# The turn between two halves of a state-space scan: from VectorE to ScalarE, and the second halves half a step later

## What is computed

```
abar = exp(dt * a)                       # per state, complex
s[t] = abar * s[t-1] + bu[t]             # a scan over 256 tokens, complex
y = Re(C s) + d * u;  y = gelu(y)
```

```
first_re = z_re[127]*cos128 - z_im[127]*sin128
first_im = z_im[127]*cos128 + z_re[127]*sin128
```

## Time and profile before

| | |
|---|---|
| time of three runs | 3233.09 us (median), 3228.68 and 3240.85 |
| the profiled execution | 3230.05 us |
| its span | 3228.7 us, 48855 instructions |
| busy: TensorE, VectorE, ScalarE, GpSimd | 3064.6, 2135.8, 1376.7, 307.3 us |
| chain that ended last | TensorE 77%, VectorE 11%, DMA 7%, ScalarE 2% |
| DMA | 632.08 MB, mean 196 GB/s |

### The profile page before, as it was taken

One profiled execution on the slowest core, in us unless ns is written; L12 is line 12 of the kernel. 1 busy time (PEld: TensorE's weight loads), 2 busy tenths in 40 slices (PEclk: granted clock), 3 DMA queues, 4 the chain that ended last, 5 costly groups with the idle time before them and its releaser, 6 DMA issues.

```text
span 3228.7 us, 48855 instructions
## 1 busy us (share of the span) xinstructions
PE 3064.6 (95%) x20283; PEld 2762.3 (86%) x20283; DVE 2135.8 (66%) x2568; ACT 1376.7 (43%) x1682; POOL 307.3 (10%) x255
## 2 busy tenths in 40 slices
PE   5799988998899999999998999999999999999998
PEld 1588878898888888888998999999999888888887
DVE  6689996677777554655787776666455755555555
ACT  2233323333353443434455564544444544444343
POOL 4547650000000000000000000000000100000000
PEclk8899999999999999999999999999999999999999
DMA  8855558867767666566555555445555556565664
GB/s 302 276 173 164 164 174 276 278 229 254 254 198 271 189 194 191 186 197 188 177 158 170 170 176 164 147 151 161 177 189 170 178 188 186 194 192 191 189 190 155
DMA packets 311483, 632.08 MB, mean 196 GB/s; under 512 B 30096, under 2 KB 34816, under 8 KB 310624
## 3 DMA queue, kind: packets, MB, share of 16 engines
q1 hardware_dynamic: 298496, 618.74, 59.4%
q10 hardware_dynamic: 11904, 5.61, 0.6%
q0 software_dynamic: 864, 4.60, 0.5%
HBM read 624.66 MB, written 4.21 MB: 195 GB/s over the span
## 4 chain that ended last, share of the span: by engine, by line
PE 77%; DVE 11%; DMA 7%; ACT 2%; issue 2%; ACTq 1%; SPq 0%; DVEq 0%
PE PS L918 13%; PE PS L905 12%; PE PS L906 11%; PE PS L907 11%; PE PS L922 7%; PE PS L934 6%; PE PS L936 6%; PE PS L935 6%; DVE wlo L1743 3%; DMA raw<-in_w_in 2%; ACT whi L2257 2%; DVE aacc L1732 2%; DMA raw<-in_w_ada 1%; DMA raw<-in_w_proj_attn 1%; DMA raw<-in_w_out 1%
## 5 line engine op out<-in xcount | busy, mean ns | idle before, releaser
L1743 DVE TENSOR_TENSOR wlo<-raw,whi 128x1024 fp32r<-128x1024 f32 x983 | 1244.4, 1270 | 920.9 <-ACT whi L2257 919.5
L2257 ACT ACTIVATE whi<-raw 128x1024 fp32r<-128x1024 f32 x983 | 1036.0, 1058 | 1386.7 <-PE PS L907 503.6
L905 PE MATMUL PS<-R,whi 128*128 128x256 f32 x4160 | 1209.5, 291 | 57.0 <-DVE wlo L1743 38.2
L906 PE MATMUL PS<-R,whi 128*128 128x256 f32 x4160 | 1189.4, 286 | 0.0
L907 PE MATMUL PS<-R,wlo 128*128 128x256 f32 x4160 | 1189.0, 286 | 0.0
L905 PEld LDWEIGHTS PS<-R,whi 128*128 128x128 f32 x4160 | 810.5, 195 | 99.4 <-issue 47.0
L906 PEld LDWEIGHTS PS<-R,whi 128*128 128x128 f32 x4160 | 811.0, 195 | 0.8 <-issue 0.7
L907 PEld LDWEIGHTS PS<-R,wlo 128*128 128x128 f32 x4160 | 810.2, 195 | 0.0
L918 PE MATMUL PS<-R,whi 128*128 128x512 f32 x1920 | 484.7, 395 | 14.7 <-DVE R L1660 8.6
L918 PEld LDWEIGHTS PS<-R,whi 128*128 128x128 f32 x1920 | 348.0, 190 | 78.6 <-issue 15.4
L934 PE MATMUL PS<-whi,R 128*128 128x512 f32 x896 | 350.1, 391 | 1.6 <-issue 0.9
(11 more groups left out here) (356 smaller groups left out, 1833.8 us busy)
## 6 DMA issues: line engine op xcount, KB each, us to landing
raw<-in_w_in SPq DMA_DIRECT2D x295, 512.0 KB, 4.1
raw<-in_w_ff SPq DMA_DIRECT2D x256, 512.0 KB, 4.0
raw<-in_w_ada SPq DMA_DIRECT2D x175, 512.0 KB, 4.8
raw<-in_w_mlp_up SPq DMA_DIRECT2D x128, 512.0 KB, 4.1
raw<-in_w_mlp_down SPq DMA_DIRECT2D x128, 512.0 KB, 3.9
raw<-in_w_out SPq DMA_DIRECT2D x64, 512.0 KB, 4.3
raw<-in_w_rnn_proj SPq DMA_DIRECT2D x32, 512.0 KB, 3.6
raw<-in_w_attn_proj SPq DMA_DIRECT2D x32, 512.0 KB, 3.7
```

The source lines that it names most:

```text
L905: pe.matmul(o, whi[:, s, c:c + P], x.operand.hi(k), start=first, stop=False, skip_group_check=True)
L906: pe.matmul(o, whi[:, s, c:c + P], x.operand.lo(k), start=False, stop=False, skip_group_check=True)
L1743: v.tensor_tensor(wlo[:, i % SPN, :], words(j), whi[:, i % SPN, :].bitcast(F32), ALU.subtract).then_inc(lo_done, 1)
L2257: a.activation(whi[:, i % SPN, :], words(j), ACT.Copy).then_inc(hi_done, 1)
```

## The change

The turn is made by ScalarE, in a side job of its own (`ssm` in the scalar program), in the even phase 2k+4: two multiplications by `-sin128` and `sin128`, then, after a wait for them, two multiply-adds with `cos128`, all on one column. It waits for the first scans (`half_done`) and signals `first_done`. VectorE's second scans of step k move from the end of the odd phase 2k+3 to the start of the even phase 2k+4, after that tick's L1743 and before the rotation of step k+1, and wait for `first_done`. GpSimd makes `-sin128` as well, one more subtraction in each half of the tables, behind a wait for VectorE's parameters, since the tile `b_` is used by these before. Nothing in TensorE's, SyncE's or GpSimd's side jobs of the stage is changed. The whole diff:

```diff
--- before.py
+++ after.py
@@ -259,7 +259,7 @@
     ptmp16 = fv(16384, 1024).rearrange("p (k n) -> p k n", k=16)
     halves = lambda a: a.rearrange("p c (h n) -> p (c h) n", h=2)
     ebase = (GB, E0)
-    cos128, sin128, z_turn, z_first = dt_, th_, a_[:, 0:2], a_[:, 2:4]
+    cos128, sin128, nsin128, z_turn, z_first = dt_, th_, b_, a_[:, 0:2], a_[:, 2:4]
 
     def etable(ft):
         o = ebase[ft // 4] + ft % 4 * 512
@@ -319,8 +319,8 @@
     evac_a = {n: sem("a_" + n) for n in ("u", "ga", "gb", "q", "k", "v", "hid", "gr", "gt", "wo")}
     evac_v = {n: sem("v_" + n) for n in ("ps", "pa", "res1", "ff", "part", "res2", "hid", "conv", "rp", "ap", "o")}
     e_done = sem("e_done")
-    bu_done, rot_done, scan_done, z_used, post_done, y_done = (sem(n) for n in (
-        "bu_done", "rot_done", "scan_done", "z_used", "post_done", "y_done"))
+    bu_done, rot_done, half_done, first_done, scan_done, z_used, post_done, y_done = (sem(n) for n in (
+        "bu_done", "rot_done", "half_done", "first_done", "scan_done", "z_used", "post_done", "y_done"))
     gelu_v, gelu_a, yg_ready = sem("gelu_v"), sem("gelu_a"), sem("yg_ready")
     bh_done, bh_copied, v_turned, v_copied = sem("bh_done"), sem("bh_copied"), sem("v_turned"), sem("v_copied")
     sc_done, max_done, exp_done, prob_done, pt_done, pt_copied, av_done, ya_hi, ya_ready = (sem(n) for n in (
@@ -1180,6 +1180,15 @@
 
         def ssm():
             for i in range(36):
+
+                r = i - 2
+                if 0 <= r < 32:
+                    z, late = zz_[r % 2], PS[:, 4 + r % 2, :].rearrange("p (c n) -> p c n", c=2)
+                    decay = mag[:, r:r + 1].broadcast_to([P, HALF])
+                    v.wait_ge(first_done, r + 1)
+                    for c in range(2):
+                        t = v.tensor_tensor_scan(z[:, c, HALF:T], decay, late[:, c, HALF:T], z_first[:, c:c + 1], ALU.mult, ALU.add)
+                    t.then_inc(scan_done, 1)
                 k = i - 1
                 if 0 <= k < 32:
                     ft, j, bank = k // 4, k % 4, 4 + k % 2
@@ -1209,18 +1218,7 @@
                     v.wait_ge(v_own, first)
                     v.tensor_tensor_scan(z[:, 0, 0:HALF], decay, bu[:, 0, 0:HALF], 0.0, ALU.mult, ALU.add)
                     v.wait_ge(v_own, second)
-                    v.tensor_tensor_scan(z[:, 1, 0:HALF], decay, bu[:, 1, 0:HALF], 0.0, ALU.mult, ALU.add).then_inc(v_own, 1)
-                    v.wait_ge(v_own, vt.one())
-                    v.tensor_scalar(z_turn, z[:, :, HALF - 1], sin128[:, k:k + 1], None, ALU.mult).then_inc(v_own, 1)
-                    v.wait_ge(v_own, vt.one())
-                    for c, op in ((0, ALU.subtract), (1, ALU.add)):
-                        t = v.scalar_tensor_tensor(z_first[:, c:c + 1], z[:, c, HALF - 1:HALF], cos128[:, k:k + 1],
-                                                   z_turn[:, 1 - c:2 - c], ALU.mult, op)
-                    t.then_inc(v_own, 1)
-                    v.wait_ge(v_own, vt.one())
-                    for c in range(2):
-                        t = v.tensor_tensor_scan(z[:, c, HALF:T], decay, bu[:, c, HALF:T], z_first[:, c:c + 1], ALU.mult, ALU.add)
-                    t.then_inc(scan_done, 1)
+                    v.tensor_tensor_scan(z[:, 1, 0:HALF], decay, bu[:, 1, 0:HALF], 0.0, ALU.mult, ALU.add).then_inc(half_done, 1)
                 yield from ssm_pause(2 * i + 1)
 
         def gelu(ft):
@@ -1941,6 +1939,22 @@
             a.wait_ge(*passed(x.name, x.i))
             a.activation(dst, banks(x), ACT.Tanh, scale=0.5).then_inc(done, 1)
 
+        def ssm():
+
+            for i in range(36):
+                k = i - 2
+                if 0 <= k < 32:
+                    last = zz_[k % 2][:, :, HALF - 1]
+                    c, sn, ns = (w[:, k:k + 1] for w in (cos128, sin128, nsin128))
+                    a.wait_ge(half_done, k + 1)
+                    a.activation(z_turn[:, 0:1], last[:, 1:2], ACT.Copy, scale=ns)
+                    a.activation(z_turn[:, 1:2], last[:, 0:1], ACT.Copy, scale=sn).then_inc(a_own, 1)
+                    a.wait_ge(a_own, at.one())
+                    a.activation(z_first[:, 0:1], last[:, 0:1], ACT.Identity, scale=c, bias=z_turn[:, 0:1])
+                    a.activation(z_first[:, 1:2], last[:, 1:2], ACT.Identity, scale=c, bias=z_turn[:, 1:2]).then_inc(first_done, 1)
+                yield from ssm_pause(2 * i)
+                yield from ssm_pause(2 * i + 1)
+
         def gelu(ft):
             g = PS[:, 6 + ft % 2, T:2 * T]
             yield
@@ -2268,6 +2282,8 @@
                 row_copy(0 if n == -33 else 1)
             if n in NORM1:
                 new.append(norm1(NORM1.index(n)))
+            if n == SSM0:
+                new.append(ssm())
             new += [gelu(ft) for ft in range(8) if n == phase_tick(14 + 8 * ft)]
             x = ends.get(n)
             if x is not None:
@@ -2431,7 +2447,10 @@
                 g.tensor_tensor(s2, c64, s64, ALU.mult).then_inc(g_own, 1)
                 g.wait_ge(g_own, gt_.one())
                 g.tensor_tensor(c2, c2, A, ALU.subtract)
-                g.tensor_tensor(s2, s2, s2, ALU.add).then_inc(e_done, 1)
+                g.tensor_tensor(s2, s2, s2, ALU.add).then_inc(g_own, 1)
+                g.wait_ge(g_own, gt_.one())
+                g.wait_ge(*v_once.at("f"))
+                g.tensor_tensor(nsin128[:, tt:tt + 16].unsqueeze(2), Es[:, :, 0:1], s2, ALU.subtract).then_inc(e_done, 1)
                 scratch["read"] = e_done, half + 1
                 yield
```

## The result

The changed kernel takes 3264.76 us (median of 4 runs, 3262.37 to 3267.92), the kernel before 3232.86 us (4 runs). The ratio is 1.0089, 95% interval 1.0075 to 1.0104: about 29 us slower. The profiled execution took 3262.68 us, 32.6 more than that of the kernel before. Forecast were 3228.5 us and a range up to 3245.

The account below looks back on a forecast made before the run. TensorE was taken to set the pace of the steady stage, with VectorE nearly full. Terms: -2.5 (VectorE freed) + 1.2 (new waits) - 0.9 - 2.0 (stage's end) = -4.2 us; forecast 3228.5 us, range 3215 to 3245.

Parts of the forecast that it names:

- the one on the margin: TensorE's L706 after the late scans: margin 0.7 us, failing where ScalarE evacuates a panel just before, 4 x 0.3 = 1.2 us.
- The bound of 8 us: Upper bound for all new waits: 8 x 1 us, a full GpSimd instruction in each of eight even ticks with partial sums.
- the clock only as a possible gain: Rival, chance 0.10: shorter gaps at the stage's end keep TensorE's clock up, 4.8 us more gain, -9 us in all, 3224.
- The thin margins: New waits before L706 where evacuations or partial sums delay the late scans: 1.2 us taken, bounds 0 and 8 x 1 us.
- the turn that outlasts its cover: Rival, chance 0.18: ScalarE's four instructions end after VectorE's L1743, delaying late scans and L706; +6 us at 2.1 us, 3239.
- taking 22 us from VectorE: Steady state-space stage: 22 us leave VectorE over 31 steps, but at most 2.5 us of TensorE's L706 waits come back.
- the margin of 0.7 us: In a normal even tick the late scans end at 268.8 us, 0.7 us before L706 at 269.56; before, 1.6.
- the turn at 1.2 us: ScalarE's four one-column instructions with handoffs: 1.2 us a step, between 0.8 and 1.34 plus two handoffs, hidden behind VectorE's L1743.
- no table load: Rival, chance 0.02, was a function table loaded around ScalarE's turn: 1.28 us each, +18 us, 3251.
- the gap of 2.88 us: TensorE's wait for L1743 at 484.99, end of the stage: forecast gone or under 1 us.
- the gain at the end: End of the state-space stage: eight partial sums gain 0.9 us, the last state's step 2.0 us (bounds 1.1 and 3.4).
- The wait in L718: Last state's unit on TensorE: waits 1.8 us for the last scans and GpSimd's 6.8 us, taking back part of the gain.

Follow-up runs that it names:

- e1: Changed kernel with ScalarE's evacuations of the u, ga and gb panels after the side jobs of their tick: 3237.89 us, ratio 1.0004 to the kernel before.
- e3: Changed kernel with the turn back on VectorE in the odd tick, only the second scans moved: 3243.06 us, ratio 1.0031 to the kernel before.
- e4: Changed kernel with ScalarE's turn in the odd phase and VectorE's second scans waiting in place there: 3266.36 us, ratio 1.0101 to the kernel before.
- e2: Changed kernel with TensorE's L706 issued half a step later, at the end of the odd tick: 3221.74 us, ratio 0.9962 to the kernel before.
- e8: e3 with e2's edit (turn on VectorE, second scans moved, L706 half a step later): 3222.53 us, ratio 0.9965 to the kernel before.
- e5: Changed kernel with the edits of both e1 and e2: 3219.89 us, ratio 0.9954 to the kernel before.
- e7: Control: kernel before with e1's edit, evacuations behind the side jobs, no turn on ScalarE: 3233.93 us, ratio 0.9999 to the kernel before.
- e6: Kernel before with e2's edit, L706 half a step later: 3228.08 us, ratio 0.9988 to the kernel before.

## Why the prediction was wrong

It forecast a gain of 4 us and a range to 3245; by the medians the kernel became 32 us slower.

- **The step that failed** is the one on the margin: "Where ScalarE evacuates a panel just before (L1942, 1.02 us), since the high part slips by it: every eighth tick, four of the nine before an even one, so 4 x 0.3 = 1.2 us." It took the evacuation for 1 us of work in the tick before. It is a wait for TensorE's unit in the same tick, issued ahead of the turn. It struck the five even ticks that end a panel, not the four before them, and cost 3.06 to 3.15 us each and not 0.3: 15.4 us by the waits alone.
- **Its upper bound fell with it.** The bound of 8 us was made of port sharing. The rows of before had the wait in plain sight: L1942 stood idle 21.4 us before 8 instructions, 2.7 us each, put down to TensorE. An instruction that idles 2.7 us in front of its own work delays all that is queued behind it.
- **The price of a TensorE wait was put too low.** The forecast had the clock only as a possible gain. In the stage it stood at 1.00 before, and no gap was over 0.92 us from 200 to 460. With the long waits of L706 it fell to the lower of its two levels, 1.2 GHz, at each of the five and once after a wait of 1.40 us. That cost 13.8 us, almost as much as the long waits. The sum had no term for it.
- **The thin margins** cost more than 1.2 us even where ScalarE is not involved: 5.0 us of L706 waits in e1, 9.9 in e3, against 2.1 before.
- **The rival that came true in part** is the turn that outlasts its cover (chance 0.18, priced +6, at most +16 with slower instructions). Its place, its queue and its victim L706 were right. Its mechanism was not: the turn took 1.16 us, and what made it late was the evacuation's wait ahead of it. e4, at 1.0101, shows that an offloaded turn is dear where nothing covers it. The rule that sends multiplications to VectorE (the Trainium skill, "ScalarE: Activation LUTs", Rules for kernel authors) gives the sign of the result, but not by the speed per element that it names as its reason: the ratios of e2 and e8, with the turn on ScalarE and on VectorE, differ by 0.03%.
- **Right:** TensorE bounds the stage and taking 22 us from VectorE returns next to nothing where L706 has its margin (e5 against e8); the margin of 0.7 us (0.8 in e1); the turn at 1.2 us; no table load appears in the steps; GpSimd's new subtraction costs nothing visible, since its tables end at 162.8 us; the gap of 2.88 us is gone, and L718 of the last state waits for GpSimd.
- **Not shown: the gain at the end.** 2.9 us were forecast and 5.3 measured after the last L706, but e7 gains 4.1 there without the change. The two waits that TensorE has there, 3.77 us for a low part at 514.41 and 4.89 in L718, are together longer than the two before, 4.67 at 477.70 and 2.88.
- The wait in L718 was larger than forecast, 4.89 us against 1.8 (changed kernel, TensorE, then GpSimd's four instructions):

```profile
527.91 1.91 PE L718 MATMUL PS<-F 128*32 128x256 f32 x4 [4.89 <-POOL F L2473]
...
518.94 3.38 POOL L2468 TENSOR_TENSOR F<-F 128x512 f32<-128x512 f32 x1 [16.28 <-DVE F L1190]
522.28 2.25 POOL L2470 TENSOR_TENSOR F<-F 128x512 f32<-128x512 f32 x1
524.61 1.58 POOL L2472 TENSOR_TENSOR F<-F 128x256 f32<-128x256 f32 x1
526.16 1.70 POOL L2473 TENSOR_TENSOR F<-F 128x256 f32<-128x256 f32 x1
```

GpSimd needed 8.9 us there instead of 6.8.

## What to carry to other kernels

Before work is moved to an idle engine, list what that engine's queue holds in the same tick and what each entry waits for: ScalarE was busy a third of the time and still the wrong place, since an evacuation ahead of the turn waited for the very unit whose follower the turn had to serve. Where a program is woven from immediate calls and running jobs, the order in the queue is that of the emission, and `once` in three places was worth 27 us. And taking work off the engine that is 97% busy brings nothing while another one sets the pace and does not wait for it (e5 against e8); it pays only where a thin margin makes the pace-setter wait (e1 against e3). Moving the consumer with the thin margin, L706, was worth more than the whole offload.

## What was not expected of the hardware

**Where GpSimd starts goes with what VectorE loses.** Before, GpSimd began right after the second scans together with VectorE's next subtraction; with the scans moved it begins beside the rotation, which reads PSUM. Groups of 180 to 460 us of e6 (scans in place), then e8 (scans moved): VectorE's low parts and GpSimd's four instructions, busy us and mean ns:

```profile
L1743 DVE TENSOR_TENSOR wlo<-raw,whi 128x1024 fp32r<-128x1024 f32 x72 | 120.7, 1683 | 2.2 <-ACT whi L2257 2.1
L2449 POOL TENSOR_TENSOR F<-F 128x512 f32<-128x512 f32 x30 | 60.6, 2018 | 96.9 <-DVE F L1222 96.9
L2451 POOL TENSOR_TENSOR F<-F 128x512 f32<-128x512 f32 x30 | 54.2, 1806 | 0.0
```

```profile
L1749 DVE TENSOR_TENSOR wlo<-raw,whi 128x1024 fp32r<-128x1024 f32 x74 | 105.8, 1434 | 10.6 <-ACT whi L2279 10.6
L2476 POOL TENSOR_TENSOR F<-F 128x512 f32<-128x512 f32 x31 | 51.1, 1647 | 0.0
...
L2474 POOL TENSOR_TENSOR F<-F 128x512 f32<-128x512 f32 x31 | 40.2, 1298 | 128.8 <-DVE F L1190 128.8
```

The low part falls from 1.68 to 1.43 us and GpSimd's first instruction from 2.02 to 1.30. That gives VectorE back 0.25 x 74 = 18 us, nearly as much as the offload's 22. Not all of it stays: the turn, which in e8 lies beside GpSimd's last instructions, takes 26.2 us in this stretch where it took 17.9 in e6. That the start is the reason is read from the order; no run moved GpSimd's start by itself. The same sharing in the other direction would explain why L2468 took 3.38 us above: it began at 518.94 beside a partial sum and a low part that VectorE ran back to back. That fits the exclusive lock that the Trainium skill describes ("SBUF — State Buffer", SBUF: two separate sides).

**Two small products in one tick are cheaper than in two.** In e2 two ticks with L707 and L718 together took 7.97 us (300.06 to 308.03), where they took 8.16 with one in each (4.04 and 4.12). Over 31 steps that is 6 us; e6, which has nothing else new, gained 4 by its ratio, with an interval from 0 to 7.
